# Stick-breaking mixers: two buffers for logarithms, terms and low parts of a pair of heads, and another order of the convolution's sums

## What is computed

```
def hybrid_mixer(u, w_in, ...):
    q, k, v, a, b, g_sb, g_conv = split(u @ w_in)      # 36 panels of 128 columns
    y_sb   = stick_breaking_attention(q, k, v) @ w_attn_out     # 8 heads of 64
    y_conv = conformer_conv(a, b, ...) @ w_conv_out
    m = sigmoid(g_sb) * y_sb + sigmoid(g_conv) * y_conv
    return m @ w_out

# attention: A[t,s] = sigmoid(z_ts) * prod over s<j<t of (1 - sigmoid(z_tj)), s < t
# conv: y = causal depthwise convolution (31 taps, 512 channels) of a * sigmoid(b);
#       silu(layernorm(y)), so mean and variance of y over the 512 channels are needed
```

## Time and profile before

| | us |
|---|---|
| runs | 2225.07, 2226.55, 2225.41 |
| median | 2225.41 |
| profiled execution, own time | 2225.93 |
| its span | 2224.1 |
| TensorE busy | 2206.4 (99%) |
| VectorE busy | 1595.8 (72%) |
| ScalarE busy | 1268.9 (57%) |
| GpSimd busy | 293.0 (13%) |

### The profile page before, as it was taken

One profiled execution on the slowest core, in us unless ns is written; L12 is line 12 of the kernel. 1 busy time (PEld: TensorE's weight loads), 2 busy tenths in 40 slices (PEclk: granted clock), 3 DMA queues, 4 the chain that ended last, 5 costly groups with the idle time before them and its releaser, 6 DMA issues.

```text
span 2224.1 us, 43598 instructions
## 1 busy us (share of the span) xinstructions
PE 2206.4 (99%) x15472; PEld 2071.9 (93%) x15472; DVE 1595.8 (72%) x2426; ACT 1268.9 (57%) x1966; POOL 293.0 (13%) x337
## 2 busy tenths in 40 slices
PE   8999999999999999999999999999999999999999
PEld 8999999999999999998888889988888889998888
DVE  6655997665566479888768867888768865686875
ACT  6444876544444368766556646766556635565662
POOL 0001662100100145220020011020010010101000
PEclk9999999999999999999999999999999999999999
DMA  6555435555555543455556555355556645446563
GB/s 228 177 188 162 158 118 167 165 172 191 160 175 183 175 161 134 144 188 188 192 167 198 196 173 164 114 180 189 189 176 194 210 158 182 161 153 199 187 208 123
DMA packets 100402, 386.58 MB, mean 174 GB/s; under 512 B 11312, under 2 KB 12464, under 8 KB 100304
## 3 DMA queue, kind: packets, MB, share of 16 engines
q1 hardware_dynamic: 99648, 383.89, 52.7%
q0 software_dynamic: 368, 1.26, 0.2%
q10 hardware_dynamic: 288, 0.12, 0.0%
HBM read 384.18 MB, written 1.05 MB: 173 GB/s over the span
## 4 chain that ended last, share of the span: by engine, by line
PE 90%; DVE 6%; ACT 2%; issue 1%; POOL 1%; DMA 0%; SPq 0%; ACTq 0%; POOLq 0%
PE bank L372 27%; PE bank L364 14%; PE bank L366 14%; PE bank L365 14%; PE bank L373 14%; DVE wlo L388 2%; DVE bank L1676 1%; ACT whi L381 1%; PE bank L988 1%; PE bank L989 1%; PE bank L990 1%; DVE at_lo L1732 0%; PE bank L1035 0%; POOL ssq L448 0%; DVE proj L1662 0%
## 5 line engine op out<-in xcount | busy, mean ns | idle before, releaser
L388 DVE TENSOR_TENSOR wlo<-raw,whi 128x1024 fp32r<-128x1024 f32 (+1 forms) x677 | 894.4, 1323 | 194.0 <-ACT whi L381 182.0
L381 ACT ACTIVATE whi<-raw 128x1024 fp32r<-128x1024 f32 (+1 forms) x677 | 745.9, 1113 | 181.0 <-PE bank L366 129.8
L372 PE MATMUL bank<-u,whi 128*128 128x512 f32 x1760 | 615.9, 393 | 0.0
L364 PE MATMUL bank<-u,whi 128*128 128x272 f32 (+1 forms) x2016 | 588.0, 292 | 7.5 <-DVE u L421 7.1
L366 PE MATMUL bank<-u,wlo 128*128 128x272 f32 (+1 forms) x2016 | 579.4, 287 | 0.0
L365 PE MATMUL bank<-u,whi 128*128 128x272 f32 (+1 forms) x2016 | 576.9, 286 | 0.0
L373 PE MATMUL bank<-u,wlo 128*128 128x256 f32 x1760 | 493.6, 280 | 0.0
L372 PEld LDWEIGHTS bank<-u,whi 128*128 128x128 f32 x1760 | 330.4, 188 | 75.1
L364 PEld LDWEIGHTS bank<-u,whi 128*128 128x128 f32 x2016 | 380.4, 189 | 9.9 <-DVE wlo L388 7.7
L365 PEld LDWEIGHTS bank<-u,whi 128*128 128x128 f32 x2016 | 380.7, 189 | 2.2 <-issue 1.7
L366 PEld LDWEIGHTS bank<-u,wlo 128*128 128x128 f32 x2016 | 380.1, 189 | 0.0
(11 more groups left out here) (309 smaller groups left out, 2973.9 us busy)
## 6 DMA issues: line engine op xcount, KB each, us to landing
raw<-w SPq DMA_DIRECT2D x552, 512.0 KB, 3.5
raw<-w SPq DMA_DIRECT2D x128, 704.0 KB, 4.1
h<-xT SPq DMA_DIRECT2D x4, 272.0 KB, 5.3
outT<-h SPq DMA_DIRECT2D x8, 128.0 KB, 4.7
consts<-cst POOLq DMA_DIRECT2D x1, 576.0 KB, 4.9
dist<-cst POOLq DMA_DIRECT2D x1, 192.0 KB, 2.7
rdist<-cst POOLq DMA_DIRECT2D x1, 192.0 KB, 4.0
sgain<-small POOLq DMA_DIRECT2D x1, 145.5 KB, 5.2
```

What stands on the lines that cost most here:

```text
L364: pe.matmul(out, w_h, x_hi, start=first, stop=False)
L372: pe.matmul(out[:, :], w_h, both, start=first, stop=False, skip_group_check=True)
L381: act.activation(whi[:, n % RING, 0:COLS[n]], raw[:, n % RING, 0:COLS[n]], ACT.Copy).then_inc(hi_ready, 1)
L388: dve.tensor_tensor(wlo[:, n % RING, 0:COLS[n]], raw[:, n % RING, 0:COLS[n]], whi[:, n % RING, 0:COLS[n]], ALU.subtract).then_inc(lo_ready, 1)
```

## The change

`ez` and `nlk` get two buffers each, laid over slots of `proj` that are free by then (V_SLOT, B_SLOT), and `lk_lo` gets two of its own. The waits for a buffer look back two heads instead of one. On ScalarE both logarithms of a pair stand in a row, ahead of terms_hi(2p), and tap_products(n[0]) comes behind terms_hi(2p). On VectorE terms(2p+1) stands ahead of terms_lo(2p), and terms_lo(2p+1) right behind split(j). In the last pair, weights_hi(7) and out_hi(6) stand ahead of the squares on ScalarE, and split(j+2) behind weights_lo(7) and out_lo(6) on VectorE. GpSimd sums its own two groups as soon as its own taps are done, then adds group 0 and group 1, each behind that group's last tap, where it used to wait for all taps first.

```diff
-            ez = sb("ez", [128, SW], f32, area)
-            nlk = sb("nlk", [128, SW], f32, area)
+            flat = proj[:, :, :].rearrange("p a t -> p (a t)")
+            ez, nlk = (flat[:, at * T:at * T + 2 * SW].rearrange("p (m c) -> p m c", c=SW) for at in (V_SLOT, B_SLOT))
...
-            lk_lo = sb("lk_lo", [128, SW], f32r, area)
+            lk_lo = sb("lk_lo", [128, 2, SW], f32r, area)
...
                 def log_terms(hd):
+                    e = ez[:, hd % 2, :]
                     act.wait_ge(z_full, H + hd + 1)
-                    if hd >= 1:
-                        act.wait_ge(nlk_done, H + hd)
+                    if hd >= 2:
+                        act.wait_ge(nlk_done, H + hd - 1)
...
                 def terms_hi(hd):
                     act.wait_ge(nlk_done, H + hd + 1)
-                    if hd >= 1:
+                    if hd >= 2:
                         act.wait_ge(c_full, H + hd - 1)
-                        act.wait_ge(lk_ready, H + hd)
+                        act.wait_ge(lk_ready, H + hd - 1)
...
                     log_terms(2 * p)
+                    log_terms(2 * p + 1)
+                    terms_hi(2 * p)
                     tap_products(n[0])
-                    terms_hi(2 * p)
-                    log_terms(2 * p + 1)
                     panel(j)
...
                     if p == PAIRS - 1:
+                        weights_hi(2 * p + 1)
+                        out_hi(2 * p)
                         for c in range(CH):
...
-                    weights_hi(2 * p + 1)
-                    out_hi(2 * p)
+                    if p < PAIRS - 1:
+                        weights_hi(2 * p + 1)
+                        out_hi(2 * p)
...
                 def terms(hd):
                     dve.wait_ge(l_done, H + hd + 1)
-                    if hd >= 1:
-                        dve.wait_ge(lk_ready, H + hd)
+                    if hd >= 2:
+                        dve.wait_ge(lk_ready, H + hd - 1)
...
                 def terms_lo(hd):
                     dve.wait_ge(lk_hi_ready, H + hd + 1)
-                    if hd >= 1:
-                        dve.wait_ge(c_full, H + hd)
+                    if hd >= 2:
+                        dve.wait_ge(c_full, H + hd - 1)
...
+                dve.wait_ge(cin_done, CH * (l + 1))
                 for p in range(PAIRS):
...
                     taps(n[1])
+                    terms(2 * p + 1)
                     terms_lo(2 * p)
                     evacuate(j)
-                    terms(2 * p + 1)
                     split(j)
+                    terms_lo(2 * p + 1)
...
                     taps(n[2])
-                    terms_lo(2 * p + 1)
                     weights_lo(2 * p)
...
-                    split(j + 2)
+                    if p < PAIRS - 1:
+                        split(j + 2)
                     weights_lo(2 * p + 1)
                     out_lo(2 * p)
+                    if p == PAIRS - 1:
+                        split(j + 2)
...
                     pool.wait_ge(pool_tap_done, total * (l + 1))
-                    pool.wait_ge(tap_done, len(DVE_ORDER) * (l + 1))
-                    for c in range(1, CH):
-                        if c > 1:
-                            pool.wait_ge(ysum_step, 3 * l + c - 1)
-                        pool.tensor_tensor(sq[:, W2], sq[:, W2] if c > 1 else proj[:, A_SLOT, W2],
-                                           proj[:, A_SLOT + c, W2], ALU.add).then_inc(ysum_step, 1)
+                    pool.tensor_tensor(sq[:, W2], proj[:, A_SLOT + 2, W2], proj[:, A_SLOT + 3, W2], ALU.add)\
+                        .then_inc(ysum_step, 1)
+                    for c in range(2):
+                        pool.wait_ge(tap_done, len(DVE_ORDER) * l + DVE_ORDER.index((c, CONV_K - 1)) + 1)
+                        pool.wait_ge(ysum_step, 3 * l + c + 1)
+                        pool.tensor_tensor(sq[:, W2], sq[:, W2], proj[:, A_SLOT + c, W2], ALU.add).then_inc(ysum_step, 1)
```

More of the change, by code:

```diff
@@ L690, in suffix_sums @@
                     both = bass.AP(whole.tensor, whole.offset + a0 + s2, [whole.ap[0], [a1 + s2 - s1 - a0 - s2, 2], [1, w2]])
-                    for n, lk in enumerate((lk_hi[:, hd % 2, :], lk_lo[:, :])):
+                    for n, lk in enumerate((lk_hi[:, hd % 2, :], lk_lo[:, hd % 2, :])):
                         pe.matmul(z[:, 0:SW], tri_r[:, :], lk[:, 0:SW], start=False, stop=False, skip_group_check=True)
@@ L1214, in log_terms @@
                 def log_terms(hd):
+                    e = ez[:, hd % 2, :]
                     act.wait_ge(z_full, H + hd + 1)
-                    if hd >= 1:
-                        act.wait_ge(nlk_done, H + hd)
-                    act.activation(ez[:, :], bank[6 + hd % 2][:, 0:SW], ACT.Abs).then_inc(az_done, 1)
+                    if hd >= 2:
+                        act.wait_ge(nlk_done, H + hd - 1)
+                    act.activation(e, bank[6 + hd % 2][:, 0:SW], ACT.Abs).then_inc(az_done, 1)
                     act.wait_ge(az_done, H + hd + 1)
-                    act.activation(ez[:, :], ez[:, :], ACT.Exp, scale=-1.0).then_inc(e_done, 1)
+                    act.activation(e, e, ACT.Exp, scale=-1.0).then_inc(e_done, 1)
                     act.wait_ge(e_done, H + hd + 1)
-                    act.activation(ez[:, :], ez[:, :], ACT.Ln, bias=one).then_inc(l_done, 1)
+                    act.activation(e, e, ACT.Ln, bias=one).then_inc(l_done, 1)
                 def terms_hi(hd):
                     act.wait_ge(nlk_done, H + hd + 1)
-                    if hd >= 1:
+                    if hd >= 2:
                         act.wait_ge(c_full, H + hd - 1)
-                        act.wait_ge(lk_ready, H + hd)
-                    act.activation(lk_hi[:, hd % 2, :], nlk[:, :], ACT.Copy).then_inc(lk_hi_ready, 1)
+                        act.wait_ge(lk_ready, H + hd - 1)
+                    act.activation(lk_hi[:, hd % 2, :], nlk[:, hd % 2, :], ACT.Copy).then_inc(lk_hi_ready, 1)
                 def weights_hi(hd):
@@ L1718, in terms @@
                     dve.wait_ge(l_done, H + hd + 1)
-                    if hd >= 1:
-                        dve.wait_ge(lk_ready, H + hd)
-                    dve.scalar_tensor_tensor(out=nlk[:, :], in0=bank[6 + hd % 2][:, 0:SW], scalar=0.0, in1=ez[:, :],
-                                             op0=ALU.max, op1=ALU.add).then_inc(nlk_done, 1)
+                    if hd >= 2:
+                        dve.wait_ge(lk_ready, H + hd - 1)
+                    dve.scalar_tensor_tensor(out=nlk[:, hd % 2, :], in0=bank[6 + hd % 2][:, 0:SW], scalar=0.0,
+                                             in1=ez[:, hd % 2, :], op0=ALU.max, op1=ALU.add).then_inc(nlk_done, 1)
                 def terms_lo(hd):
                     dve.wait_ge(lk_hi_ready, H + hd + 1)
-                    if hd >= 1:
-                        dve.wait_ge(c_full, H + hd)
-                    dve.tensor_tensor(lk_lo[:, :], nlk[:, :], lk_hi[:, hd % 2, :], ALU.subtract).then_inc(lk_ready, 1)
+                    if hd >= 2:
+                        dve.wait_ge(c_full, H + hd - 1)
+                    dve.tensor_tensor(lk_lo[:, hd % 2, :], nlk[:, hd % 2, :], lk_hi[:, hd % 2, :], ALU.subtract)\
+                       .then_inc(lk_ready, 1)
                 def weights_lo(hd):
```

## The result

The changed kernel takes 2231.11 us, the median of 12 runs (2228.79 to 2233.68), against 2225.90 for the kernel before (12 runs on the same chip, 2225.07 to 2226.55). The ratio, which is that of the means, is 1.0026, with a 95% interval of 1.0018 to 1.0033. By the medians it is slower by 5.2 us, where 1.4 was forecast, and outside the range that was given. The profiled execution took 2233.62 (span 2231.7), 7.6 us more span than before.

A forecast was written before the change was run, and what follows sets the result against it. TensorE was taken as the bound, busy 2206.4 of 2224.1 us, with at most 5.2 us to gain. Terms -2.2 - 1.2 + 1.5 + 3.3 = +1.4 gave a median of 2226.8 us, range 2222.6 to 2230.0.

The forecast's parts named there:

- TensorE's granted clock stays full: Sign expected in the changed profile: no slice below the top tenth, the longest wait being 7.1 us at the start.
- suffix_sums(3): TensorE's wait for lk_lo(3) in each mixer: removed by the two buffers, -1.1 each, -2.2 us.
- weighted_values(7): TensorE's hole at the last head in both mixers: removed by putting its weights first, -1.2 us.
- variance: Before the variance's product: late squares make new waits of 0.7 and 0.8 in the two mixers, +1.5 us.
- mean: Before the mean of the convolution's output: GpSimd's late last tap lengthens the wait about 1.6 per mixer, +3.3 us.
- The 1.3 of hold-up: GpSimd's last tap and three sums: time lost to VectorE's split and low parts, 1.3 us, between 1.1 and 2.2.
- The term of nothing for suffix_sums(6): First head of a pair: lk_lo(2p) comes 0.52 us later behind nlk(2p+1), said to cost nothing.
- the sum is in time: Rival: early nlk(6) and a free port remove the hole before the mean; -3.7, 2221.7 us; chance 0.17.
- GpSimd is passed over: Rival: VectorE keeps the port over two instructions, so the last sum ends later; +4.8, 2230.2 us; chance 0.12.
- The buffers don't free suffix_sums: Rival: GpSimd collisions keep lk_lo(2) or lk_lo(3) late, 2.2 not saved; +3.6, 2229.0 us; chance 0.13.
- This part by itself loses 0.3: Last head's weights first, both mixers: -1.2 at the last head against +1.5 for late squares, loss 0.3 us.
- Nothing else changed would end near 323.7: GpSimd's own tiles summed first, alone: three sums end near 323.7, ahead of TensorE at 324.7, removing the mean's hole.

The follow-up runs named there:

- f_filled: The changed kernel with 17 TensorE products that nobody reads put ahead of its wait for the mean; 2229.10 us.
- e_product_first: The changed kernel with tap_products(n[0]) moved back between the pair's two logarithms; 2222.22 us.
- b_own_sum: The kernel before with only GpSimd's own tiles summed first; 2227.19 us.
- c_last_head: The kernel before with only the last head's weights ahead of the squares and the split of panel 35 behind out_lo(6); 2228.62 us.
- d_product_behind: The kernel before, single buffers kept, with only a pair's first tap products moved behind terms_hi(2p); 2236.30 us.
- e2: The changed kernel with tap_products(n[0]) behind both logarithms but ahead of terms_hi(2p); 2224.19 us.
- h_squares_old: The changed kernel with the product between the logarithms and ScalarE's squares back ahead of the last head's weights; 2220.62 us.
- its variant: The changed kernel with the product between the logarithms, the squares in their old place and GpSimd's old sums; 2222.12 us.
- a_buffers: The kernel before with only the buffers, both logarithms in a row and the product behind terms_hi; old sums, squares and last split; 2231.76 us.

## Why the prediction was wrong

**The step that failed** is the last sentence of its last part: "TensorE's granted clock stays full". The sum had no term for the clock. The term was 2.3 us in the median, by the one run without a fall, and 3.9 in the profiled execution; f_filled, with the same order and no fall, gives 2.2 in the median and 3.8 in the profiled span. The reason given, that the wait of 7.1 us at the program's start is followed by no low slice, rested on a row that can't show it. The timeline of the kernel before has the answer, behind that very wait:

```profile
7.11 0.56 PE L364 MATMUL bank<-u,whi 128*128 128x272 f32 x1 [7.11 <-DVE u L421]
...
8.15 0.43 PE L365 MATMUL bank<-u,whi 128*128 128x272 f32 x1
8.38 0.43 PE L366 MATMUL bank<-u,wlo 128*128 128x272 f32 x1
...
10.84 0.29 PE L365 MATMUL bank<-u,whi 128*128 128x272 f32 x1
10.96 0.29 PE L366 MATMUL bank<-u,wlo 128*128 128x272 f32 x1
```

0.23 apart and 0.43 long until 10.6, then 0.12 to 0.13 apart and 0.29 long: TensorE started at half speed, although the granted clock of 8 to 11 us reads 1.00 in the windows. Read before the prediction, these rows would have made a hole of 2.1 us, which was forecast in the first mixer with one of about 2.9 (1.3 + 1.6) in the second, a risk with a price of its own. The Trainium skill (TensorE: Matmul & The Clock Gate, Part 1: The HAM clock gate) says that idling halves TensorE's clock and sustained work restores it, and puts the penalty of ramping up at under 1% of a typical span. The runs agree with both: 3.9 us is 0.2% of this span. They are also more than any part of the change could gain.

**The terms of the four forecast holes** came out nearly right as sums over both mixers; the waits that the forecast put at nothing were a second failed step. Per hole, lost time against the kernel before:

| term | forecast | measured |
|---|---|---|
| suffix_sums(3) | -2.2 | -2.2 |
| weighted_values(7) | -1.2 | -1.2 |
| variance | +1.5 | +1.6 |
| mean | +3.3 | +3.2 |
| suffix_sums(6), weighted_values(2) | 0 | +1.3 |
| clock | 0 | +2.3 in the median, +3.9 in the profile |

The chain behind the mean is the one described: product behind the wait of lk_hi(6) for nlk(6), GpSimd's last tap behind the product, three sums behind that. But it is made up otherwise: +2.1 in the first mixer (2.57 lost for 0.50) and +1.2 in the second (2.46 for 1.29), where 1.6 was forecast in each. That the two errors cancel is luck. Less the 0.4 that this execution started late, nlk(6) ran at 320.1, not 319.0: VectorE gained 0.6 on the kernel before, less than the 0.87 that was taken for the least. The last sum ended at 326.4, not 325.6, and TensorE was ready at 323.9, not 323.6. The 1.3 of hold-up that was taken for the whole of GpSimd's end was 1.0. The reading behind it was loose in one place: the split of 1.21 in the earlier trace rows was not alone, since the tap of 283.06 ran beside it, and it was the tap that grew longer.

**The term of nothing for suffix_sums(6)** failed by the sentence "0.52 later for the first head, which the suffix sums of that head did not wait for anywhere: nothing". That they did not wait doesn't say by how much: in the second mixer lk_lo(6) came only 0.24 ahead of them. With nlk(7) 0.51 ahead of it, a longer lk_lo(6) and a VectorE that gained less than was taken, they waited 0.74. Moving the product ahead of the wait again (e_product_first) was enough to make this wait vanish.

**Of the rivals**, "the sum is in time" described another kernel, e_product_first (2222.2 for 2221.7). "GpSimd is passed over" was right on the side and wrong on the cause: the sums were held up by 1.0 us over the earlier trace rows, not by the 1.5 more per mixer that it asked for. "The buffers don't free suffix_sums" had the right thing in the wrong head: 2 and 3 were free, 6 was not. A time slower by over 0.2% had been given a chance of 0.12; the measured ratio is 1.0026.

**Parts alone.** "This part by itself loses 0.3" (the second) held for the first mixer and failed in the second, where 2.02 of idle stood for 0.6 (0.8 lost): the delay of GpSimd's sums by VectorE was not counted for it. "Nothing else changed would end near 323.7" (the third) held, but the sum took the hole before the mean as given back in full, and b_own_sum shows 1.1 of its 1.8 us waiting again at weighted_values(7).

What stays open: why an equal hole brings the clock down in one execution and not in another, and by which steps the late products kept VectorE from gaining what was taken.

## What to carry to other kernels

Price a hole in front of TensorE twice: its own length, and what the clock may do behind it. In this kernel, where TensorE is 99% busy, the second was 2.3 for a hole that lost 2.5 itself, and the spacing of equal products shows it where the page's clock row can't. That a chain doesn't wait today says nothing of its slack: read how early it comes before putting a delay of it at nothing. When a reorder pulls one chain forward, list the small instructions that slide behind its wait, and follow each to the last engine that needs it: here products of 0.5 us, one in the last pair, moved ahead of the wait again, turned a loss of 5.2 us into a gain of 3.9. And test the parts apart: the best version keeps the two buffers, the new sums and the later split, and drops the move of the squares.

## What the runs showed of the hardware

The clock fell behind idle stretches of TensorE as short as these: 1.39 us (b_own_sum, in 6 of 11 runs), 2.02 (c_last_head, 8 of 11), 2.10 and 2.95 (d_product_behind), 2.40 and 2.29 (the changed kernel, 11 of 12). The counts go by each run's mean clock; which hole a fall stood behind is known for the profiled execution alone. No fall was seen in the kernel before, whose longest hole in the mixers is 1.12, nor in the kernels with holes up to 0.83 there (e, e2, h and its variant). And a hole need not bring it down: none was seen behind 2.40 (a_buffers, first mixer), 1.55 and 2.11 (d_product_behind), nor in any of the twelve profiled executions behind a hole of 1.32 to 1.53 that all kernels have later in the program, in the kernel before this one:

```profile
PE bank L486 <- POOL ssq L448: 1.3, 1, 1.3
```

So 1.39 with a fall and 1.53 without stand beside each other. The profiled stretches at 1.2 GHz lasted 3.4 or 6.8 us, and the runs with a fall were slower than those of the same kernel without by 2.1 (b_own_sum), 1.1 (c_last_head) and 2.3 (the changed kernel, by its median).

GpSimd and VectorE slow each other. Of GpSimd's sums: two sums took 1.62 in the kernel before, 2.10 in e_product_first and 2.63 in the changed kernel; three sums of squares 2.58 in h_squares_old (x3 at 328.99), 3.39 in the changed kernel and, in the second mixer, 2.51 in h_squares_old and 4.64 in c_last_head. VectorE's lk_lo, 0.60 in the median, took 0.93 and 0.95 in the two last pairs of the changed kernel, beside GpSimd's last tap and first sum. The Trainium skill (SBUF — State Buffer, "Who interferes with whom") has the shared port as an exclusive lock. The trace of c_last_head agrees with it: 2.1 more than 2.51, beside two splits of 2.44 together, each with two inputs in SBUF.
